# One slab multiplied ahead of its norm's factor, a convolution on three engines with its sums in PSUM, and one low part on GpSimd

## What is computed

```python
def hybrid_mixer(n, w_in, ...):
    z = jnp.einsum("bsd,de->bse", n, w_in)
    x_lru, g_lru, a_glu, b_glu = jnp.split(z, ...)
    xc = depthwise_conv(x_lru, lru_conv_w, lru_conv_b, ...)
    h_fwd = rg_lru(xc, ..., False); h_bwd = rg_lru(xc, ..., True)
    y_lru = (h_fwd + h_bwd) * jax.nn.gelu(g_lru)
    glu = a_glu * jax.nn.sigmoid(b_glu)
    c = depthwise_conv(glu, conf_conv_w, conf_conv_b, (15, 15))
    y_conv = jax.nn.silu(group_layer_norm(c, conf_norm_g, conf_norm_b))
    y = jnp.concatenate([rms_norm_2(y_lru, beta_lru), rms_norm_2(y_conv, beta_conv)], axis=-1)
    return jnp.einsum("bse,ed->bsd", y, w_out)

x = first_block(...)
h = x + hybrid_mixer(rms_norm_2(x, mix_norm_g), ...)
h = h + peer_ffn(rms_norm_2(h, ffn_norm_g), peer_w_q, peer_sub_keys, peer_u, peer_v)
out = rms_norm_2(h, final_norm_g)
```

## Time and profile before

| what | value |
|---|---|
| median of 3 runs | 3993.97 us (3993.76 to 3994.91) |
| the profiled execution | 3992.91 us, its span 3991.2 us |
| TensorE busy | 3860.4 us, 97% of the span |
| VectorE busy | 2588.1 us, 65% |
| ScalarE busy | 1596.8 us, 40% |
| GpSimd busy | 594.3 us, 15% |

### The profile page before, as it was taken

The page is one execution under the profiler, slowest core; times in us unless marked ns, Lnnn a source line. Parts: engine busy times, 40 slices in busy tenths (PEclk is TensorE's granted clock), DMA queues, the critical chain, the costliest instruction groups (busy, mean ns, idle before and its releaser), DMA issues. The chain is left out here.

```text
span 3991.2 us, 54574 instructions
## 1 busy us (share of the span) xinstructions
PE 3860.4 (97%) x19554; PEld 3237.1 (81%) x19554; DVE 2588.1 (65%) x4756; ACT 1596.8 (40%) x2237; POOL 594.3 (15%) x572
## 2 busy tenths in 40 slices
PE   7999999999999989998999999999999999999998
PEld 6888786877788878886667888668999999988886
DVE  6642776766663466427854324768998888687887
ACT  3221335335322232225863222543355666533333
POOL 1100000000110011000000000000125554233332
PEclk9999999999999999998999999989999999999999
DMA  7632421321652256323012222212359999899997
GB/s 285 227 133 95 147 95 37 121 93 67 235 212 101 104 182 224 131 90 94 1 64 89 101 95 84 75 43 103 134 185 340 359 343 350 310 353 351 355 356 271
DMA packets 140840, 702.12 MB, mean 176 GB/s; under 512 B 18791, under 2 KB 20166, under 8 KB 95182
## 3 DMA queue, kind: packets, MB, share of 16 engines
q1 hardware_dynamic: 66734, 424.29, 29.2%
q0 software_dynamic: 73952, 275.81, 19.2%
HBM read 637.06 MB, written 59.80 MB: 175 GB/s over the span
## 5 line engine op out<-in xcount | busy, mean ns | idle before, releaser
L112 DVE TENSOR_TENSOR w_lo<-raw,w_hi 128x2048 fp32r<-128x2048 f32 x324 | 742.7, 2292 | 699.9 <-ACT w_hi L104 698.1
L130 PE MATMUL ps<-x_hi,w_hi 128*128 128x512 f32 (+1 forms) x2768 | 1031.7, 373 | 9.7 <-DVE w_lo L112 2.8
L131 PE MATMUL ps<-x_lo,w_hi 128*128 128x512 f32 (+1 forms) x2768 | 1022.7, 369 | 0.0
L132 PE MATMUL ps<-x_hi,w_lo 128*128 128x512 f32 (+1 forms) x2768 | 1022.4, 369 | 0.0
L104 ACT ACTIVATE w_hi<-raw 128x2048 fp32r<-128x2048 f32 x331 | 632.6, 1911 | 648.6 <-PE ps L132 421.5
L130 PEld LDWEIGHTS ps<-x_hi,w_hi 128*128 128x128 f32 x2768 | 521.1, 188 | 81.3 <-issue 9.0
L131 PEld LDWEIGHTS ps<-x_lo,w_hi 128*128 128x128 f32 x2768 | 521.0, 188 | 68.4
L132 PEld LDWEIGHTS ps<-x_hi,w_lo 128*128 128x128 f32 x2768 | 520.7, 188 | 68.3
L2594 PE MATMUL ps<-w_hi,px_gh 128*128 128x512 f32 x768 | 299.0, 389 | 1.7 <-issue 1.3
L2594 PE MATMUL ps<-w_lo,px_gh 128*128 128x512 f32 x768 | 298.8, 389 | 0.0
L2594 PE MATMUL ps<-w_hi,px_gl 128*128 128x512 f32 x768 | 298.8, 389 | 0.0
(11 more groups left out here) (433 smaller groups left out, 5688.3 us busy)
## 6 DMA issues: line engine op xcount, KB each, us to landing
raw<-in_slabs SPq DMA_DIRECT2D x331, 1024.0 KB, 4.8
ada_ring<-in_w_ada POOLq DMA_DIRECT2D x160, 512.0 KB, 5.5
act_dram<-px_act SPq DMA_DIRECT2D x64, 384.0 KB, 6.7
gate_dram<-ps_g SPq DMA_DIRECT2D x12, 2048.0 KB, 11.6
px_g<-gate_dram POOLq DMA_DIRECT2D x32, 768.0 KB, 7.9
px_ai<-act_dram POOLq DMA_DIRECT2D x64, 384.0 KB, 6.5
h_dram<-h SPq DMA_DIRECT2D x2, 2048.0 KB
h<-h_dram SPq DMA_DIRECT2D x2, 2048.0 KB, 8.1
```

The costliest lines, as they stand in the source:

```text
L112: nc.vector.tensor_tensor(k.wlo[:, c % 2, :], k.raw[:, c % 2, :], k.whi[:, c % 2, :].bitcast(F32), ALU.subtract).then_inc(k.raw_free, 1)
L130: mm(out, hi, rhs_hi, start=start, stop=False)
L131: mm(out, hi, rhs_lo, start=False, stop=False)
L132: return mm(out, lo, rhs_hi, start=False, stop=stop)
```

## The change

It has three parts.

*The first slab.* `Early` multiplies the mixer's slab 0 during the end of the feed-forward stage with h times gain, without 1/rms, tile by tile as the y tiles come. ScalarE makes the high part (`early.high`) behind each tile's square, VectorE the low part (`early.low`) behind each tile's add, TensorE six products a tile into banks 0 and 1, with the eight sums after the seventh tile and the spread after the eighth. The unread products of `norm_total` and `norm_start` go here. In the mixer's input stage TensorE begins with slab 1; VectorE multiplies slab 0's result with 1/rms (a copy of the spread factor to SBUF, then one product of 128 x 1024) after its norm and ahead of slab 2's low part.

*The convolution.* TensorE keeps tile 3 alone. VectorE does tiles 1 and 2, 62 instructions, with the running sums in PSUM banks 4 and 5 and the last tap written to SBUF. GpSimd does tile 0: a product with the tap's weight, then a dependent add, 12 taps in the input stage after `glu` and 19 in the branches. The gate products use four banks instead of six. `acc3` also waits for GpSimd, since GpSimd's products lie in the buffer that it writes.

*PEER.* GpSimd makes the first key slab's low part; VectorE's place for it goes, and its next split waits until that buffer is free.

```diff
+class Early:
...
+    def high(self, act, n):
...
+        k.nc.scalar.activation(self.xh[:, m, :], k.h[:, m, :], ACT.Copy, scale=self.gain[:, m:m + 1])\
+            .then_inc(self.s["hi"], 1)
+    def low(self, ve, n):
+        k, m = self.k, self.order[n]
+        ve.wait_ge(self.s["hi"], n + 1)
+        k.nc.vector.scalar_tensor_tensor(self.xl[:, m, :], k.h[:, m, :], self.gain[:, m:m + 1],
+                                         self.xh[:, m, :].bitcast(F32), ALU.mult, ALU.subtract).then_inc(self.s["lo"], 1)
+    def products(self, pe, total, rb, sums_at, spread_at):
...
+        for n, m in enumerate(self.order):
+            if n == sums_at:
+                pe.wait_ge(k.n["summed"], KT * k.norms + KT - 1)
...
+            pe.wait_ge(self.s["lo"], n + 1)
+            for half, b in enumerate(self.banks):
+                last = mm3(k, bank(k, b), self.f % 2, m * 256 + half * P, self.xh[:, m, :], self.xl[:, m, :],
+                           n == 0, n == KT - 1)
+            last.then_inc(k.slab_used if n == KT - 1 else self.s["used"], 1)
+        if spread_at == KT:
+            norm_spread(k, pe, rb, k.norms + 1)
@@ stage_ffn: scalar, vector, tensor
                 norm_square(k, act, n, m, sil, total)
-            if f > 0:
+                if early:
+                    early.high(act, n)
+                    if n == 4:
+                        split_hi(k, 0, f + n_in + n_out + 1)
+            if f > 0 and not early:
...
                     norm_add(k, ve, n - 1, sil, total)
+                if early and n > 0:
+                    early.low(ve, n - 1)
             norm_add(k, ve, KT - 1, sil, total)
+            if early:
+                early.low(ve, KT - 1)
...
-                if last_one:
+                if last_one and early:
+                    pe.wait_ge(k.n["h"], KT * k.norms + 3)
+                    early.products(pe, total, SUM_BANK, KT - 1, KT)
+                elif last_one:
                     norm_total(k, pe, total)
@@ the convolution
-BY_PE = 12
 EARLY = (8, 20, 28)
-VE_TAPS = [(tap, t) for tap in range(TAPS) for t in range(3) if t < 2 or tap < TAPS - BY_PE]
+EARLY_GPSIMD = 12
+VE_TAPS = [(tap, t) for tap in range(TAPS) for t in (1, 2)]
...
+    sums = bank(k, 3 + t)
...
-        V.scalar_tensor_tensor(acc[:, t, :], glu[:, t, tap:tap + T], col(k, "cconv_w", 4 * tap + t),
-                               acc[:, t, :], ALU.mult, ALU.add).then_inc(mx["tap"], 1)
+        V.scalar_tensor_tensor(sums if tap < TAPS - 1 else acc[:, t, :], glu[:, t, tap:tap + T],
+                               col(k, "cconv_w", 4 * tap + t), sums, ALU.mult, ALU.add).then_inc(mx["tap"], 1)
+def gpsimd_tap(k, gp, mx, glu, acc, tap):
...
+        gp.wait_ge(mx["gtap"], 2 * tap - 1)
+        G.tensor_scalar(acc[:, 3, :], glu[:, 0, tap:tap + T], col(k, "cconv_w", 4 * tap), None, ALU.mult)\
+            .then_inc(mx["gtap"], 1)
+        gp.wait_ge(mx["gtap"], 2 * tap)
+        G.tensor_tensor(acc[:, 0, :], acc[:, 3, :], acc[:, 0, :], ALU.add).then_inc(mx["gtap"], 1)
@@ stage_mixer_in: gpsimd, tensor, scalar, vector
+        @blk.gpsimd
+        def _(gp):
+            gp.wait_ge(s["pad"], 1)
+            gp.wait_ge(s["glu"], 1)
+            for tap in range(EARLY_GPSIMD):
+                gpsimd_tap(k, gp, mx, glu, acc, tap)
...
-            norm_start(k, pe, f)
-            step(0, 0, True)
-            step(0, 1)
+            step(0, 1, True)
+            pe.wait_ge(s["z0"], 1)
             two_step(pe, 6, step, 2)
...
-            for c in range(4):
+            for c in range(1, 4):
                 step(0, c)
...
             norm_low(k, ve, sig, norm[0], norm[1], SUM_BANK)
+            V.tensor_copy(sig[:, 3, :], bank(k, SUM_BANK)).then_inc(s["rcopy"], 1)
+            ve.wait_ge(k.slab_used, f + 3)
+            ve.wait_ge(s["rcopy"], 1)
+            V.tensor_tensor(z[:, 0:2, :], bank(k, 0, 2 * T).rearrange("p (a t) -> p a t", a=2),
+                            sig[:, 3:4, :].to_broadcast([P, 2, T]), ALU.mult).then_inc(s["z0"], 1)
             split_lo(k, 0, f + 2)
@@ stage_branches: gpsimd, tensor, scalar, vector
+            for tap in range(EARLY_GPSIMD, TAPS):
+                gpsimd_tap(k, gp, mx, glu, acc, tap)
...
-                if n >= 6:
-                    pe.wait_ge(s["gate"], n - 5)
-                mm(bank(k, n % 6), wgt[:, dr, j, t, :], xc[:, t, :], start=True, stop=True).then_inc(s["mm"], 1)
+                if n >= 4:
+                    pe.wait_ge(s["gate"], n - 3)
+                mm(bank(k, n % 4), wgt[:, dr, j, t, :], xc[:, t, :], start=True, stop=True).then_inc(s["mm"], 1)
...
-            for j in range(BY_PE):
-                tap = TAPS - BY_PE + j
-                pe.wait_ge(s["diag"], j + 1)
-                mm(bank(k, 6), diag[:, j, :], glu[:, 2, tap:tap + T], start=j == 0, stop=j == BY_PE - 1)\
...
-                elif t == 2:
-                    pe.wait_ge(s["comb"], 1)
+                elif t == 0:
+                    pe.wait_ge(mx["gtap"], 2 * TAPS - 1)
...
             act.wait_ge(s["dused"], TAPS)
+            act.wait_ge(mx["gtap"], 2 * TAPS - 1)
             A(acc[:, 3, :], bank(k, 7), ACT.Identity, bias=col(k, "cconv_b", 3)).then_inc(s["acc3"], 1)
...
-            V.tensor_tensor(acc[:, 2, :], bank(k, 6), acc[:, 2, :], ALU.add).then_inc(s["comb"], 1)
@@ stage_peer: gpsimd, vector
+            gp.wait_ge(s["sc"], 1)
+            split_lo_gpsimd(k, gp, f + 2)
             for c in range(HEADS - 1):
...
-                split_lo(k, 3 * i, n + 1)
+                    split_lo(k, 3 * i, n + 1)
                 best_of_pairs(i, c)
+                if c == 0:
+                    ve.wait_ge(k.raw_free, n + 4)
                 split_lo(k, 3 * i, n + 2)
```

More of the change, by code:

```diff
@@ L373, in norm_spread, with norm_high @@
     last.then_inc(k.n["r"], 1)
-def norm_high(k, act, stage, shift, between=None):
-    for t in range(KT):
-        act.wait_ge(k.n["scaled"], KT * k.heads + t + 1)
+def norm_high(k, act, stage, shift, between=None, tiles=range(KT), ahead=0):
+    for t in tiles:
+        at = KT * (k.heads + ahead) + t + 1
+        act.wait_ge(k.n["scaled"], at)
         k.nc.scalar.activation(k.xh[:, t, :], stage[:, t % 2, :], ACT.Identity,
@@ L382, in norm_high, with norm_low @@
             between()
-def norm_low(k, ve, stage, gain, shift, rb, permuted=False, between=None):
+def norm_low(k, ve, stage, gain, shift, rb, permuted=False, between=None, tiles=range(KT), ahead=0):
     V = k.nc.vector
-    ve.wait_ge(k.n["r"], k.heads + 1)
+    done = KT * (k.heads + ahead)
+    ve.wait_ge(k.n["r"], k.heads + ahead + 1)
     def scaled(t):
         if t > 1:
-            ve.wait_ge(k.n["lo"], KT * k.heads + t - 1)
+            ve.wait_ge(k.n["lo"], done + t - 1)
         src, r, dst = k.h[:, t, :], bank(k, rb), stage[:, t % 2, :]
@@ L397, in scaled @@
         V.scalar_tensor_tensor(dst, src, gain[:, t:t + 1], r, ALU.mult, ALU.mult).then_inc(k.n["scaled"], 1)
-    scaled(0)
-    for t in range(KT):
-        if t + 1 < KT:
+    scaled(tiles[0])
+    for t in tiles:
+        if t + 1 in tiles:
             scaled(t + 1)
-        ve.wait_ge(k.n["hi"], KT * k.heads + t + 1)
+        ve.wait_ge(k.n["hi"], done + t + 1)
         V.scalar_tensor_tensor(k.xl[:, t, :], stage[:, t % 2, :], 0.0 if shift is None else shift[:, t:t + 1],
@@ L406, in norm_low, with __init__ @@
             between()
+class Early:
+    def __init__(self, k, ctx, gain, order, f, banks, own):
+        self.k, self.gain, self.order, self.f, self.banks = k, gain, order, f, banks
+        made = scratch(k, ctx, "early_x", [P, 2, KT, T], F32R) if own else None
+        self.xh, self.xl = (made[:, 0], made[:, 1]) if own else (k.xh, k.xl)
+        self.s = signals(k, ctx, "early_", ("hi", "lo", "used"))
+    def high(self, act, n):
+        k, m = self.k, self.order[n]
+        act.wait_ge(k.n["h"], KT * k.norms + n + 1)
+        k.nc.scalar.activation(self.xh[:, m, :], k.h[:, m, :], ACT.Copy, scale=self.gain[:, m:m + 1])\
+            .then_inc(self.s["hi"], 1)
+    def low(self, ve, n):
+        k, m = self.k, self.order[n]
+        ve.wait_ge(self.s["hi"], n + 1)
+        k.nc.vector.scalar_tensor_tensor(self.xl[:, m, :], k.h[:, m, :], self.gain[:, m:m + 1],
+                                         self.xh[:, m, :].bitcast(F32), ALU.mult, ALU.subtract).then_inc(self.s["lo"], 1)
+    def products(self, pe, total, rb, sums_at, spread_at):
+        k, mm = self.k, self.k.nc.tensor.matmul
+        slab_ready(k, 0, self.f)
+        for n, m in enumerate(self.order):
+            if n == sums_at:
+                pe.wait_ge(k.n["summed"], KT * k.norms + KT - 1)
+                for b in range(NB):
+                    last = mm(bank(k, SUM_BANK, 1, b), total[:, b * P:(b + 1) * P], k.ones[:, 0:1],
+                              start=b == 0, stop=b == NB - 1)
+                last.then_inc(k.n["summed"], 1)
+            if n == spread_at:
+                norm_spread(k, pe, rb, k.norms + 1)
[5 more added lines that the diff above has]
```

(9 more changed lines are left out.)

33 lines of the change are left out of this document (18 added, 15 removed).

## The result

The changed kernel takes 4024.72 us (median of 6 runs, 4020.85 to 4026.02), the kernel before 3994.44 beside it: a ratio of 1.0074, 95% interval 1.0063 to 1.0084. It is **some 30 us slower**, where 4004 was forecast and 4012 was the upper end. The profiled execution took 4024.53 us, its span is 4022.8 against 3991.2. One kernel of the experiments, the one with GpSimd's tap 0 alone, ran two of its ten executions at a lower granted clock (0.84) in 4346 and 4347 us; its median and ratio are those of the other eight.

The account below looks back on a forecast made before the run. TensorE, heading the chain of waits with 27% of the span, was taken to bound the kernel. 0 + 7.5 + 3.5 - 0.5 = +10.5 us gave 4003.4 in the profile, 4004 for the median; range 3987 to 4012.

Parts of the forecast that it names:

- Part 1: First slab ahead of the norm's factor: stage starts 5.6 us late, one slab less; 0 in total, ends -1.7 and +1.
- end of -1.7: First slab, mixer's input stage: the favourable limit of the forecast of 0, 1.7 us faster.
- its gain ends at slab 2's split: Mixer's input stage: the first slab's gain stops where TensorE idles 3.6 us for slab 2; 1.7 gained go to the clock.
- Part 2, input stage: Convolution in the mixer's input stage: GpSimd's taps hold VectorE's recurrence convolution; +7.5 us, ends 0 and +10.
- one for one: Recurrence's convolution: VectorE and GpSimd instructions alternate singly, holding VectorE for GpSimd's remaining 7.2 us.
- Part 2, branches: Convolution in the branches: ScalarE's copy of tile 3 waits for GpSimd's 19 taps; +3.5 us, ends -2.3 and +9.
- the multiply is 0.52 to 0.61: GpSimd's convolution taps: the multiply of 512 columns, priced from a one-input cast of 1.06 us for 1024, in us.
- I take 1.95: GpSimd's convolution: us for each later tap, multiply, dependent add and two gaps, chosen from 1.67 to 2.2.
- the taps are dear: Convolution rival: 2.3 us or more a GpSimd tap, input stage held 10; +15 to +22 us, chance 0.14.
- Part 3: PEER's first key slab: GpSimd's split removes a 2.85 us idle, the clock takes 1.7 back; -0.5 us, ends -2.2 and 0.
- for being right: Signs: stage near 2481.9, slab 2 near 2498.4, 12 instructions some 15 us, input stage 5 to 10 later, copy X+49, keys gapless.
- signs of being wrong: Recurrence's 12 instructions still 8 us, GpSimd's adds under 1 or over 1.6 us, or slab 2 starting before 2495.

Follow-up runs that it names:

- parts 1 and 3: The first-slab and PEER changes on the kernel before, with the convolution as before: 3996.19 us, ratio 1.0003.
- the version ahead of both: First-slab and PEER changes on the kernel before, old convolution, slab 2's split reordered, slabs 2, 4, 6 in other banks, unread products added: 3989.98 us, ratio 0.9988.

## Why the prediction was wrong

*Part 1* was right: 0 forecast, -0.8 in the trace, no measurable change alone. The stage's start came 4.9 us later (5.6 forecast), slab 2's first product at 2499.07 (2498.4 forecast) after 3.68 us of idle, and the clock took what was left (0.54 to 0.64 in the next 2 us). But that the clock falls there was in part luck: in the three traces where it fell at slab 1, as with parts 1 and 3, the gated product came 2.4 us earlier against the split ahead, past the end of -1.7. The sentence "its gain ends at slab 2's split" held, since slab 2 starts 16.4 us after the stage in either case; in the version ahead of both it starts 14.8 us after it, and the gated product comes 1.6 to 3.2 us earlier.

*Part 2, input stage*: +7.5 forecast, +8.6. The mechanism is shown: 13.87 us with 12 taps beside it, 8.03 without GpSimd, 8.02 with five taps that end before. VectorE's instructions with two SBUF operands take turns with GpSimd's, though not one for one, as the sum had it: in each round of a product and an add, some 3.4 us, three of VectorE's end, after 0.74, 1.77 and 1.17 us (0.75 each before). The size came out near by errors that cancel: at 3.03 us a tap GpSimd worked beside the whole run, not for 7.2 us of it, but the 12 are held by half a microsecond each in the mean (5.84 over 12), and the four multiplies, with one SBUF operand, were not counted as held, but took 2.74 more. (The Trainium skill, SBUF — State Buffer, "Who interferes with whom", names `tensor_scalar` among the operations that can take the shared pair in a two-port mode. These rows agree, and so do the 1 - a² steps, 2.18 instead of 1.23; taps with their sum in PSUM were not held, as it also says.)

*Part 2, branches* is **the step that failed**: "+3.5", by "the multiply is 0.52 to 0.61" and "I take 1.95" a tap. The step scaled a cast by its columns to price an arithmetic instruction of another form, which no row showed. Measured: 1.57 a product, 3.03 a tap undisturbed. 19 taps were 37 us in the sum; at 3.03 they are 57.6, and they took 70.1, from 2578.65 to 2648.77, of which 12.5 held by VectorE (11.6 forecast). The rival "the taps are dear" had the right outcome for another reason: the gaps between dependent instructions, on which it rested, are 0.08 to 0.1 us, and its +15 to +22 stopped short. That the price is what failed is shown by the two-operation form: at 2.15 a tap the two stages lose 6.8 and 4.2 us, against 7.5 and 3.5 forecast. That both sums are 11.0 is in part luck, since 2.15 is still above 1.95 and the four multiplies were not counted. The Trainium skill, GPSIMD Engine Reference, "3.1", would have the product at 1.03 cycles an element with one input, as an estimate 0.44 us; no form measured here reaches that (0.70, 1.04, 1.50, 1.57), and the measurement decides. Its two-input figure, as an estimate 1.11 us, agrees with the slope of the rows: from 512 to 2048 columns the time grows from 1.27 to 4.60 us, 2.17 ns a column, so 1.11 us for 512 and 0.16 that don't grow.

*Part 3*: -0.5 forecast; -0.8 in the changed kernel, +0.3 alone. The trade of a 2.85 us idle for one of 3.7 at half clock was as described.

*The end of the program* was not in the sum. In the traces all kernels with part 2 are 3.1 to 5.8 us longer after GpSimd's last split, those without it -0.6 to 2.3. TensorE's longest waits from there on in the changed kernel (us in total, times, longest):

```profile
PE ps L2674 <- DVE px_gl L3017: 2.9, 2, 2.6
```

Its longest is 2.6 us, ahead of the first values' product, where before has 1.33 us; what follows is 1.9 us longer too. Even the kernel with one tap on GpSimd has it. Ahead of that product VectorE waits 2.51 and 2.45 us for rows that are gathered, where before it waited 0.77 and 0.64; why they arrive later was not tried and stays open.

*The signs.* Of those for being right all came but one: against its start the input stage ends 2.9 us later (95.60 against 92.70 to X), not 5 to 10, which the prediction's own sum did not give either (7.5 less the 5.6 of the later start). None of the signs of being wrong came, and none of them named GpSimd's product.

The chances: 0.44 was on slower by over 0.2%, which it was. The range ended at 4012 because the dear case, at 0.14, was left mostly outside.

## What to carry to other kernels

A price on GpSimd is for one form of one instruction: before a chain of 60 dependent ones is moved there, it needs a row of that very form, since one operation instead of two made 1.57 us out of 0.70. Work given to GpSimd beside VectorE is not free for VectorE either: put it beside instructions with an operand in PSUM, and let it end before the first run of two-SBUF-operand ones, as with five taps, where that stage lost nothing and the seven moved taps came back in the next. And work out first what the change would give if the moved work cost nothing (here 1.6 us up to the out projection, nothing measurable in the whole): that ceiling decides whether its price is worth a bet. Where a step shortens a wait of TensorE, look at the clock behind the next one; an earlier split and unread products in that gap together gave what the step alone had not.

## What was not expected of the hardware

- GpSimd's product of 512 columns by a scalar takes 1.57 us with a column operand, 1.50 with a constant, 0.70 with a second operation (adding zero), and 1.04 as a product of two operands, one of them broadcast.
- VectorE's product with a column, one SBUF operand, is held by GpSimd: 4.66 us for four instead of 1.92; its four scans 6.99 instead of 4.57.
- Products of two columns depend on the clock like wide ones: 32 of them took 3.70 us at a granted clock of 1.00, and 6.99 at 0.50, behind an idle of 5.80 us.
- With the same instructions on TensorE up to slab 2, its clock fell behind the idle of 2.31 us ahead of slab 1 in three traces (idle ahead of slab 2 then 2.1 us), and behind one of 3.7 us ahead of slab 2 in six.
